# Second in-projection: choices in parts, four index buffers, sums in four banks; first expert slabs refilled by halves; query Grams behind the widest level

## The reference

```python
# block 1: the delta rule, per chunk: a triangular solve, queries against keys, a state carried on
a_mat = where(strict, einsum('bhnid,bhnjd->bhnij', k_beta, k) * decay, 0.0)
qk = where(incl, einsum('bhnid,bhnjd->bhnij', q, k) * decay, 0.0)
state = state * gl_c + einsum('bhcd,bhce->bhde', kd_c, v_new)
# block 1: experts; each chooses cap = 64 of the 512 tokens
top_val, top_idx = lax.top_k(swapaxes(aff, 1, 2), cap)
xs = h[top_idx]
ye = (silu(xs @ w_gate) * (xs @ w_up)) @ w_down          # 16 experts, 1024 -> 2048 -> 1024
# block 2: the in-projection; its parts a_q, a_ckv, a_iq, a_ik, a_iw, a_gate, b_q, b_f, b_i, b_gate
h = einsum('bsd,dc->bsc', x, w_in)
# block 2: the index score of each key, and the choice of the best 128 of the keys
score = einsum('bqh,bqhs->bqs', iwb * w_scale, relu(einsum('bqhd,bsd->bqhs', iqb, ik) * idx_scale))
_, sel = lax.top_k(where(admissible, score, -inf), k_sel)
# block 2: the recurrence with its decays, then a norm over the head width and a gate
state = exp(b_last) * state + einsum('bhsk,bhsv->bhkv', kn * exp(b_last - bn), vn)
o_b = rms_norm(o_b, hgrn_norm_g) * silu(b_gate)
```

## Time and profile before

| | before |
|---|---|
| median of 3 runs | 2397.63 us (2395.41 to 2397.66) |
| the profiled execution's own time | 2399.99 us |
| its span, first to last instruction | 2398.2 us |
| mean granted TensorE clock, as a share of full | 0.987 |
| PE busy | 2220.2 us (93% of the span) |
| DVE, ACT, POOL busy | 883.2, 534.8, 170.6 us |
| moved by DMA | 488.07 MB, mean 204 GB/s |

### The profile page before, as it was taken

How to read it: one execution, slowest core, us unless ns; L and a number is a source line. 1 busy time by engine, 2 the same in 40 slices (tenths; PEclk the granted TensorE clock), 3 DMA queues, 4 the chain that set the end, 5 groups by cost and what they waited for, 6 DMA issues and landing times. The chain is left out here.

```text
span 2398.2 us, 28551 instructions
## 1 busy us (share of the span) xinstructions
PE 2220.2 (93%) x11793; PEld 1117.8 (47%) x11793; DVE 883.2 (37%) x1559; ACT 534.8 (22%) x996; POOL 170.6 (7%) x166
## 2 busy tenths in 40 slices
PE   8999999999999999969999898989898978998998
PEld 4445554467767754444343333333333325454444
DVE  2327757665767640140101010101010103465684
ACT  2435645532222240010000000000000002232323
POOL 0000000033333300000000000000000000021000
PEclk9999999999999999989999999999999999999999
DMA  6202110011011151428999999999999995311210
GB/s 242 71 35 73 36 36 18 9 37 36 20 28 37 28 193 63 184 106 361 428 428 428 428 428 428 428 428 428 427 427 428 428 428 195 110 36 37 73 53 36
DMA packets 93540, 488.07 MB, mean 204 GB/s; under 512 B 9894, under 2 KB 36932, under 8 KB 68836
## 3 DMA queue, kind: packets, MB, share of 16 engines
q1 hardware_dynamic: 93411, 486.25, 50.0%
HBM read 482.82 MB, written 3.41 MB: 203 GB/s over the span
## 5 line engine op out<-in xcount | busy, mean ns | idle before, releaser
L1562 PE MATMUL PS<-R 128*64 128x512 f32 x1024 | 231.4, 600 | 34.0 <-DMA R<-w_up 25.2
L1562 PE MATMUL PS<-SL,R 128*64 128x512 f32 x1024 | 228.5, 598 | 24.2 <-DMA SL<-w_gate 16.7
L2048 PE MATMUL PS<-HT,SL 128*128 128x512 f32 x384 | 168.6, 594 | 0.0
L1562 PEld LDWEIGHTS PS<-R 128*64 128x64 f32 x1024 | 70.6, 137 | 185.7 <-issue 128.1
L1753 DVE TENSOR_TENSOR HT<-HT,PS 128x512 f32<-128x512 f32 x32 | 20.6, 683 | 368.5 <-PE PS L1562 368.5
L1562 PEld LDWEIGHTS PS<-SL,R 128*64 128x64 f32 x1024 | 73.1, 138 | 177.4 <-issue 130.1
L1589 PE MATMUL PS<-SL,HT 128*64 128x512 f32 x256 | 114.4, 594 | 13.5 <-ACT HT L1678 6.2
L1589 PE MATMUL PS<-R,HT 128*64 128x512 f32 x256 | 114.3, 594 | 12.5 <-ACT HT L1678 7.0
L1758 DVE COPY HT<-PS 64x512 f32<-64x512 f32 x16 | 10.9, 683 | 303.6 <-PE PS L1590 303.6
L669 PE MATMUL PS<-HT,SL 128*128 128x512 f32 x256 | 114.9, 603 | 0.8 <-PEq L437 0.8
L1590 PE MATMUL PS<-SL,HT 128*64 128x512 f32 x256 | 114.9, 596 | 0.0
(11 more groups left out here) (396 smaller groups left out, 3458.0 us busy)
## 6 DMA issues: line engine op xcount, KB each, us to landing
R<-w_gate SPq DMA_DIRECT2D x32, 2048.0 KB, 35.4
SL<-w_gate SPq DMA_DIRECT2D x32, 2048.0 KB, 33.6
SL<-w_up SPq DMA_DIRECT2D x32, 2048.0 KB, 32.7
R<-w_up SPq DMA_DIRECT2D x32, 2048.0 KB, 33.0
SL<-w_down SPq DMA_DIRECT2D x32, 2048.0 KB, 35.4
R<-w_down SPq DMA_DIRECT2D x31, 2048.0 KB, 27.7
SL<-w_in SPq DMA_DIRECT2D x18, 2048.0 KB, 8.0
X<-w_in SPq DMA_DIRECT2D x16, 512.0 KB, 3.9
```

Source lines behind the costliest of these rows:

```text
L1562: m = pe.matmul(banks[n][half * CAP:(half + 1) * CAP, :], XC[x // 2 % 2][:, 2 * j + k, toks], w[:, k, (2 * half + n) * 512:(2 * half + n + ...
L2048: m = pe.matmul(bank_[:, :], slab(i % 2)[:, k, j * P:(j + 1) * P], hT[:, k, :], start=(k == 0), stop=(k == KD - 1))
```

## The change

Gated-delta stage: the query Grams of the next pair go behind `widest_X` instead of ahead of it, and DVE's state updates are divided by direction, the first ahead of its last level, the second behind it.

Experts: the first gather works by single chunks, with a bank for each of them (eight gathers, eight evacuations), and alternates with half slabs. Slabs 8 to 11, which take the place of the first four, are loaded in two halves, the first when PE has used the first half of the old slab (`E7["half"]`).

Second in-projection: `rel` has four buffers from item 8 on. The items 16 to 23 stand behind the units 18 to 21. `choose(1)` is cut into rounds 0 to 9 and, behind unit 16's weighings, 10 to 15; `choose(3)` into rounds 0 to 4 ahead of the multiplications of the norm, and 5 to 15 behind them. `c_turn` stands behind unit 21, ACT's squares too; the four sums have a bank each. POOL multiplies the keys ahead of the queries.

The counts of the semaphores follow from these (`2 * q + 4` becomes `2 * q + 8` and so on); such lines, and those where only the name of a buffer or bank changes, are left out below.

```diff
@@ -1107,8 +1107,9 @@
...
                             gram_k(n + 1, 1)
+                        widest_X(n)
+                        if n + 1 < len(PAIRS):
                             gram_q(n + 1)
-                        widest_X(n)
@@ -1304,9 +1307,11 @@
...
                     if scan and goes_on(n - 1):
-                        states(n - 1)
+                        states(n - 1, 0)
                     if inv:
                         level(n, NL - 1)
+                    if scan and goes_on(n - 1):
+                        states(n - 1, 1)
@@ -1345,6 +1350,7 @@
...
         ring_in = [sem(f"ring_in{i}") for i in range(NR)]
+        first_bank = lambda c: PS[(4, 5, 6, 7, 2, 3, 4, 5)[c]][:, 0:P]
         GB, UB, TB, DB, OB = (PS[0], PS[1]), (PS[2], PS[3]), PS[4], PS[5], (PS[6], PS[7])
@@ -1375,6 +1381,13 @@
...
             src = w[x, f0:f0 + rows, :].rearrange("(p k) n -> p (k n)", p=P)
+            if NR <= r < NR + 4:
+                for k in range(2):
+                    eng.wait_ge(*((E7["used"], r - NR + 1) if k else (E7["half"], r - NR + 1)))
+                    cols = slice(k * 2 * D, (k + 1) * 2 * D)
+                    eng.dma_start(RING[r % NR][:, cols], src[:, cols]).then_inc(ring_in[r % NR], 16)
+                return
             if r < NE * PER - 1:
@@ -1520,13 +1533,12 @@
...
-                def first_gather(j):
+                def first_gather(j, k):
                     pe.wait_ge(E6["sel"], 1)
-                    for k in range(2):
-                        for t in range(NT):
-                            m = pe.matmul(PS[4 + j][:, k * P:(k + 1) * P], h2[:, t, 256 * j + k:256 * (j + 1):2],
-                                          Sel[0][:, t, :], start=(t == 0), stop=(t == NT - 1))
+                    for t in range(NT):
+                        m = pe.matmul(first_bank(2 * j + k), h2[:, t, 256 * j + k:256 * (j + 1):2],
+                                      Sel[0][:, t, :], start=(t == 0), stop=(t == NT - 1))
                     m.then_inc(E7["xg"], 1)
@@ -1541,26 +1553,30 @@
...
                     r = x * PER + part
-                    pe.wait_ge(ring_in[r % NR], 16 * (r // NR + 1))
+                    halves_ = 1 if r >= NR and r % NR < 4 else 0
+                    pe.wait_ge(ring_in[r % NR], 16 * (r // NR + 1 + halves_))
                     return RING[r % NR][:, :]
...
                     for j in range(4):
-                        if x == 0 and part == 0:
-                            if j == 0:
-                                first_gather(0)
-                            if j < 3:
-                                first_gather(j + 1)
-                            pe.wait_ge(E7["xc"], j + 1)
+                        opening = x == 0 and part == 0
+                        if opening and j == 0:
+                            first_gather(0, 0)
                         w = arrive(x, part + j).rearrange("p (k n) -> p k n", k=2)
...
                             first, last = j == 0 and k == 0, j == 3 and k == 1
+                            if opening:
+                                if not last:
+                                    first_gather(j + k, 1 - k)
+                                pe.wait_ge(E7["xc"], 2 * j + k + 1)
                             for n in range(2):
...
                                                   w[:, k, (2 * half + n) * 512:(2 * half + n + 1) * 512], start=first, stop=last)
+                            if opening and k == 0:
+                                m.then_inc(E7["half"], 1)
                         m.then_inc(E7["used"], 1)
@@ -1659,14 +1675,13 @@
...
-                for j in range(4):
-                    act.wait_ge(E7["xg"], j + 1)
-                    nc.scalar.activation(XC[0][:, 2 * j:2 * j + 2, :], PS[4 + j][:, 0:256].rearrange("p (k n) -> p k n", k=2),
-                                         ACT.Copy).then_inc(E7["xc"], 1)
+                for c in range(KD):
+                    act.wait_ge(E7["xg"], c + 1)
+                    nc.scalar.activation(XC[0][:, c, :], first_bank(c), ACT.Copy).then_inc(E7["xc"], 1)
                 for x in range(NE):
@@ -1823,7 +1844,8 @@
...
-        BIAS0, LEVEL0, TURN, SCAN0, SUMS = 1, 8, 17, 18, 22
+        BIAS0, LEVEL0, TURN, SCAN0, C_TURN, SUMS = 1, 8, 17, 18, 21, 22
+        SUM_BANK = (PS[2], PS[3], PS[6], PS[7])
         QLAT0 = UNIT["a_gate", 1]
@@ -1838,7 +1860,7 @@
...
-        DOTS = {12: 3, 13: 3, 14: 2, 16: 4, 17: 4, 21: 3, 22: 3, 23: 2}
+        DOTS = {12: 3, 13: 3, 14: 2, 16: 4, 17: 4, 18: 2, 19: 2, 20: 2, 21: 2}
@@ -1879,11 +1901,10 @@
...
                     g(nc.gpsimd.tensor_tensor(lower, lower, blocks(kk, s_)[:, :, 0:s_], ALU.mult), E12["K"])
-                pool.wait_ge(E12["e"], 1)
+                pool.wait_ge(E12["e"], 2)
+                g(nc.gpsimd.tensor_tensor(kk, kk, FB[1], ALU.mult), E12["kd"])
                 pool.wait_ge(E12["Q"], NL)
                 g(nc.gpsimd.tensor_tensor(bq, bq, FB[0], ALU.mult), E12["qe"])
-                pool.wait_ge(E12["e"], 2)
-                g(nc.gpsimd.tensor_tensor(kk, kk, FB[1], ALU.mult), E12["kd"])
@@ -2014,9 +2035,9 @@
...
                     pe.wait_ge(E12["sq"], h + 1)
-                    if h >= 2:
-                        pe.wait_ge(E12["rs"], h - 1)
-                    pe.matmul(PS[2 + h % 2][:, :], ones, sq12[h], start=True, stop=True).then_inc(E12["ss"], 1)
+                    if h == 2:
+                        pe.wait_ge(E10["relu"], len(ITEMS))
+                    pe.matmul(SUM_BANK[h][:, :], ones, sq12[h], start=True, stop=True).then_inc(E12["ss"], 1)
@@ -2058,12 +2079,13 @@
...
                         scan(n - SCAN0)
+                    if n == C_TURN:
+                        c_turn()
+                    if QLAT0 <= n < QLAT0 + 4:
+                        q_lat(n - QLAT0)
                     if n == SUMS:
-                        c_turn()
                         for h in range(4):
                             sums(h)
-                    if QLAT0 <= n < QLAT0 + 4:
-                        q_lat(n - QLAT0)
                     for m in dots_after(n):
@@ -2162,16 +2184,9 @@
...
                             a(cp(KDt[:, 4 * u:4 * u + 4, :], PS[4 + u % 2][:, :].rearrange("p (a d) -> p a d", a=4), ACT.Copy), E12["te"])
-                    if n == SUMS:
+                    if n == C_TURN:
                         act.wait_ge(E9["ct"], 1)
                         a(cp(cT, PS[4][:, :], ACT.Copy), E9["ct_evac"])
-                        act.wait_ge(E12["oe"], NT)
-                        for h in range(4):
-                            a(cp(sq12[h], OGl[:, h, :], ACT.Square), E12["sq"])
-                        nc.scalar.preload_act_table_set("natural_log_exp_and_others")
-                        for h in range(4):
-                            norm(h)
-                        nc.scalar.preload_act_table(ACT.Silu)
                     if QLAT0 <= n < QLAT0 + 4:
@@ -2179,9 +2194,20 @@
...
                         act.wait_ge(E10["dot"], m + 1)
-                        if m >= 2:
+                        if 2 <= m < 8:
                             act.wait_ge(E10["used"], m - 1)
-                        a(cp(rel[m % 2][:, 0:W], PS[6 + m % 2][:, 0:W], ACT.Relu, scale=0.125), E10["relu"])
+                        elif m >= 8:
+                            act.wait_ge(E10["used"], max(8, m - 3))
+                        a(cp(rel(m)[:, 0:W], PS[6 + m % 2][:, 0:W], ACT.Relu, scale=0.125), E10["relu"])
+                    if n == SUMS - 1:
+                        act.wait_ge(E12["oe"], NT)
+                        for h in range(4):
+                            a(cp(sq12[h], OGl[:, h, :], ACT.Square), E12["sq"])
+                    if n == SUMS:
+                        nc.scalar.preload_act_table_set("natural_log_exp_and_others")
+                        for h in range(4):
+                            norm(h)
+                        nc.scalar.preload_act_table(ACT.Silu)
                     if LEVEL0 < n <= LEVEL0 + NL - 2:
@@ -2272,9 +2298,9 @@
...
                     if h == 0:
-                        v(ts(sc, rel[n % 2][:, 0:W], w, None, ALU.mult), E10["used"])
+                        v(ts(sc, rel(n)[:, 0:W], w, None, ALU.mult), E10["used"])
                     else:
-                        v(stt(sc, rel[n % 2][:, 0:W], w, sc, ALU.mult, ALU.add), E10["used"])
+                        v(stt(sc, rel(n)[:, 0:W], w, sc, ALU.mult, ALU.add), E10["used"])
@@ -2317,7 +2343,7 @@
...
                     weigh(m)
-                choose(1)
+                choose(1, 0, 10)
@@ -2340,13 +2366,16 @@
...
                     if n == SUMS:
+                        choose(3, 0, 5)
                         for h in range(4):
...
                         weigh(m)
-                        if ITEMS[m] == (3, 7):
-                            choose(3)
+                    if n == TURN - 1:
+                        choose(1, 10, 16)
+                    if n == SUMS:
+                        choose(3, 5, 16)
```

25 lines of the change are left out of this document (15 added, 10 removed).

## The result

| | before | after |
|---|---|---|
| median | 2397.64 us (2395.41 to 2398.62) | 2372.85 us (2370.76 to 2376.22) |
| the profiled execution's own time | 2399.99 us | 2371.33 us |
| span | 2398.2 us | 2369.5 us |

The ratio is 0.9895 with a 95% interval of 0.9884 to 0.9907: 24.8 us faster (22 to 28). Forecast were 26.3 us less and a time of 2371.3; the range was 2365 to 2380.

The account below looks back on a forecast made before the run. PE was taken to bound the gated-delta stage and second in-projection, the weight stream the experts. Terms 20.7 + 3.2 + 2.4 = 26.3 us off the 2397.6 median gave 2371.3 us, range 2365 to 2380.

Parts of the forecast that it names:

- The turn of the keys and the dots behind it: Second in-projection: four buffers free ACT, PE's wait goes and the clock returns; 15.7 us become 5.1, 10.6 less.
- POOL's order: Second in-projection: keys multiplied first frees DVE's addition, so the exponential ends 3.1 us earlier; PE's wait shrinks by 1.9 us.
- SUMS: Second in-projection, 2247.75 to 2263.25: earlier squares, four banks and moved dots remove waits and half clock; 8.2 us less.
- Gated-delta: Gated-delta stage, seven pair borders: query Grams cover PE's wait for DVE's last level; 3.2 us less, bounds 2.5 and 4.
- the gain of a border: Gated-delta stage: 0.45 us taken for each of seven borders, from a 0.57 us wait and a new stall of 0 to 0.15.
- The argument on the states: Gated-delta stage: the level would stand behind eight state updates (3.03 us); divided, only four (1.5 us) are ahead of it.
- First slabs: Expert opening: single-chunk gathers and half slabs start the full weight stream earlier; 2.4 us less, bounds 0 and 2.9.
- The finer alternation: Expert opening: switching between single-chunk gathers and half slabs costs some 0.1 us at each of four more switches.
- the count: Expert opening: ask times less 4.90 us per slab ahead give the stream's start, 1086.9 before and 1084.0 after; 2.9 us.
- POOL in the way of DVE: Rival, second in-projection: POOL's moved query multiplication blocks DVE, dots 14 and 15 wait some 2.5 us; 2373.8 us, chance 0.12.
- ACT was untied: Rival denied here, second in-projection: some relu still stands behind a choice, so the buffers don't untie ACT; about 2389, chance 0.05.
- no piece of a choice became a stall: Rival denied here, second in-projection: pieces of the choices, 34 us, hold ACT and then PE; about 2405, chance 0.03.

Follow-up runs that it names:

- x_pairhalf: The changed kernel with the first gathers by two chunks as before, slabs still refilled by halves; 2374.11 us (one run).
- x_nohalf: The changed kernel with the old opening of the experts (two-chunk gathers, whole slabs refilled); 2375.18 us (4 runs), ratio 0.9905 to the kernel before.
- x_pool: The changed kernel with POOL's two multiplications in the old order, queries first; 2382.35 us (one run).
- x_warm: The changed kernel with two-chunk gathers, half slabs and 12 useless matmuls on PE ahead of the gathers; 2375.12 us (4 runs), ratio 0.9908 to the kernel before.

## Why the prediction was right, and where it was not

**The turn of the keys and the dots behind it: 10.6 forecast, 10.2 measured.** The stretch from the first turn to unit 18 was to shrink from 15.7 to 5.1 us; it is 5.50 (2175.12 to 2180.62): 2.67 for the turn instead of 2.4, and 2.83 for the dots instead of 2.7. The view that carried it was PE's wait together with ACT's own wait in the earlier trace rows: the engine that PE waited for was not busy but stuck. The clock came back as assumed (1.00). What the step had too simple is the cause: it gave the whole to the buffers. The runs show two edits that each remove the link; undoing both brings back 8.9 of the 10.2.

**POOL's order: 1.9 forecast, 1.98 measured** between the starts of units 16 and 17 (11.74 us before, 9.76 after). The rule of the Trainium skill that the prediction weighed (page "SBUF — State Buffer", section "SBUF: two separate sides": two SBUF inputs on DVE beside a POOL instruction that reads SBUF) is borne out by the pair 3.82 and 0.69 us. Undone in the new kernel the same edit costs 3.6, with the clock.

**SUMS: 8.2 forecast, 8.3 measured** from unit 18 to unit 24 (2200.91 to 2272.69 before; that stretch is 8.3 shorter after, with all dots counted). Predicted was that ACT is at the squares in time, that the four sums go through, and that the multiplications behind 5 rounds of choice have cover; the sums are one row of 3.60 us, and the multiplications end at 2243.8 with no wait of PE for DVE or ACT anywhere behind. Of it 2.5 us are the banks; the remaining 5.8, the earlier squares and the moved dots, were not tried apart.

**Gated-delta: 3.2 forecast, 4.4 measured**, above the bound of 4. The place, the number of borders and the cover were right. The term that was mis-sized is the gain of a border: I took 0.57 less up to 0.15 for a new stall at `widest_X`. There is no new stall, and rows that start without a wait also take 1.04 us instead of 1.11: 7 x (0.57 + 0.07) = 4.5. The argument on the states was needless: half or whole ahead of the level, it ends in time now that the Grams cover it.

**First slabs: 2.4 forecast, 0.0 (give or take 0.3) measured**, the lower bound. Right was the earlier first ask (6.1 us behind the first gather; forecast 5.7, before 9.7), and that the slab behind the halves, slab 12, then sets the stream. Two terms were wrong. The finer alternation costs 1.3 us instead of 0.4, all of it in the ask of slab 12, which the count had left where it was: with the measured ask the count gives 21.0 - 9.8 = 11.2 us before and 29.3 - 19.6 = 9.7 after, so 1.6 us instead of 2.9. And the count took the time from ask to landing as the same for every slab: it was 8.5 us for the slab that set the stream before, 9.9 for slab 12 after, which takes 1.4 of the 1.6. So in the profiled pair slab 12 landed 0.2 us earlier, measured from the first gather; in the mean of the profiles it is 0.8, and at slab 187 it is nothing. What makes this delay differ by up to 2 us, and what takes the rest of the lead, is open.

**The sum.** 20.5 + 4.4 + 0.0 = 24.9 of the 26.3 forecast, and 24.8 by the medians: two errors, 1.2 too little and 2.4 too much, that partly cancel. So part of how close the whole came is luck; the mechanisms of the second in-projection, but for what unties ACT, and of the gated-delta stage were right. Of the rivals, POOL in the way of DVE was not seen: POOL's last multiplication ended at 2173.79 and the first weighing started at 2174.58, so the two never met, and the rounds of the choice beside POOL took 0.43 and 0.41 us as without it; ACT was untied, and no piece of a choice became a stall; the one wait left is the 0.6 us of a dot for its relu.

No version tried is clearly better than the change. The kernel with half slabs but without the single-chunk gathers (x_pairhalf) or with neither (x_nohalf) is its equal in the changed stage; the simplest that should keep the gain is the change without its expert part and without the division of the states, which was not run as one kernel.

## What to carry to other kernels

Where an engine waits for another that is idle, look at what that one's own order is stuck on: here a wait of 8.8 us on TensorE was a buffer on ScalarE, held by a choice on VectorE, and either a buffer more or a cut in the long piece was enough. Count a wait at more than its length if the clock falls behind it; the same 1.98 us cost 1.98 in one kernel and 3.6 in another. And an earlier start of a stream is worth only what the pace of its asks then holds: finer pieces asked earlier gained 2.8 us at once, then came at 348 GB/s because TensorE freed them no faster, and the lead was gone some 30 us later.

## What the hardware showed that was not expected

- In the opening both half and whole slabs moved at the pace at which they were asked, 341 to 377 GB/s, with the DMA engines busy 95 to 100% of the time. A busy share near 1 did not mean that the queue was full: at 421 GB/s it was 0.99.
- With a full queue the halves moved at 421 GB/s and whole slabs at 428: 0.08 us for each further DMA. Into a nearly empty queue a half took 5.1 to 5.4 us from issue to landing and a whole slab 8.5 to 9.1, where the bytes alone are 2.45 and 4.90 us at 428 GB/s.
- The granted clock fell in x_pool behind an idle time of 1.98 us (0.66 in the 5 us there) and not in the kernel before behind the same idle time at the same place. In x_warm it fell to 0.50 some 2 us into busy work, though it had been at 0.95 in the 2 us before and at 0.99 to 1.00 earlier.
- The gated-delta stage and the second in-projection repeat to 0.1 us where their code is the same; a stretch of small matmuls ahead of them (48 records, 5.44 or 7.55 us) and the rest of the first 475 us differ by up to 5 us from run to run, with the clock. A smaller difference than that in the whole time of one run says nothing on this kernel; in one of these two stages it does.
